# A hybrid decoder layer on one core: the depthwise convolution's taps are moved into earlier projection units, and the samples' taps become one product and one sum per channel tile

## The chip, the cores and the metric

One core of one Trainium2 chip. The time is that of one execution on the device, in microseconds. Five engines work side by side and meet only at semaphores: TensorE (PE, matmuls), VectorE (DVE), ScalarE (ACT), GpSimd (POOL) and SyncE (SP, which issues loads). A kernel's instructions stand in a fixed order on each engine.

## The reference

One layer for a prompt of 1024 tokens and for 8 samples of 4 tokens, with width 1024. What the change touches is the mixer, whose input projection gives q, k, v (512 columns each), and value and gate of a convolution module (512 channels each):

```python
z = h @ p["w_in"]
q, k, v, a, gate = jnp.split(z, [...], axis=-1)
...
attn = combine_branches(outs, lses).reshape(B, T, ATTN_WIDTH)
u = a * jax.nn.sigmoid(gate)
u_ctx = jnp.concatenate([conv_ctx, u], axis=1)          # 30 rows of context in front
c = causal_dwconv(u_ctx, p["conv_w"]) + p["conv_b"]     # width 31, per channel
c = jax.nn.silu(layer_norm(c, p["ln_conv_g"], p["ln_conv_b"]))
mix = jnp.concatenate([rms_norm(attn, ...), rms_norm(c, ...)], axis=-1)
x = x + rms_norm(mix @ p["w_out"], p["g_post_mix"])
```

Behind the mixer come a cross-attention to 256 memory tokens, and a gated feed-forward part with a convolution of width 3. Everything is float32.

## The kernel before

All code is written by hand per engine, with named semaphores: `mark(name, key)` counts one up, `at(name, key)` is the count to wait for.

**Tiles.** Channels lie on the 128 partitions, tokens along the free dimension. The 1056 tokens (1024 of the prompt, 32 of the samples) are worked in 3 chunks of 352 columns. `U` holds the gated values of the prompt, [128, 4 channel tiles, 30 + 1024], `US` those of the samples, [128, 4, 8, 30 + 4], and `C` the convolution's output, [128, 4, 1056]. `cw` holds the taps' weights, [128, 31, 4], so that two taps of a channel tile lie 16 bytes apart.

**The input projection** is a list of 20 units (`order_in`), each one 128 output columns: gate 0, value 0 (`"a"`), gate 1, value 1, and so on to value 3, then four k, four v and four q units. Matmuls are split in three products for accuracy (`whi`, `wlo`), so that a unit has 72 matmuls. `wlo` is a GpSimd subtraction per unit. A unit's three banks are 0 to 2 or 3 to 5 by turns, so TensorE can write a bank when the unit two before has been read from it: gate banks by ScalarE's sigmoid into `U`, value banks by VectorE's product into `U` and `US` (L1563, L1567), k, v and q banks by ScalarE's copies (L570). Behind the unit after a k or v unit TensorE transposes the tile (L997) into banks 6 and 7, in three groups, of which the third needs bank 6 again; VectorE copies them out (`tok_kv`, L1548 and L1550).

**The convolution** is a list of jobs on VectorE, ordered by channel tile, tap and group, `"p"` for the 1024 prompt columns and `"s"` for the 32 sample columns. Each job multiplies the shifted input by the tap's weight and adds it to `C`, so it waits for the job of the same group one tap before. `conv(14)` issues 14 jobs behind each of the twelve k, v and q units (L1571), `conv(2)` two behind each attention step (L1607), until all 248 are done, which is behind the 40th step.

**The attention steps** follow the units: 66 turns for 64 pairs of a query tile i (0 to 7) and a head. Step s has a score product of i + 1 key blocks on TensorE, VectorE's masked maximum (L1484) and its negation (L1594), ScalarE's exponential (L589), TensorE's transposes (L997), ScalarE's copies (L597, L600), and TensorE's product with V, whose result VectorE scales (L1606). On TensorE the order is score s, transposes s - 1, product with V of s - 2. Behind the steps come the sample attention (where `KTS` is first written), the memory part, and the layer norm of `C`.

Memory is placed by hand. `h1hi` and `h1lo`, the split input, are read by all 20 units; later tiles such as `KTS` lie over them.

Of the kernel before, what the change touches and what calls it, by code (L numbers as in the profile page):

```python
# [10 lines left out]
AX = mybir.AxisListType  # L11

P = 128
D = 1024
NT = D // P
SEQ = 1024
BD, TD = 8, 4
NS = BD * TD
NTOK = SEQ + NS
# [8 lines left out]
CT = CC // P  # L28
KW = 31
PAD = KW - 1  # L30
# [73 lines left out]
class Signals:  # L104
# [14 lines left out]
    def mark(self, name, key, by=1):  # L119
        n = SHARED.get(name, name)  # L120
        self.now[n] = self.now.get(n, 0) + by
        assert (name, key) not in self.noted, (name, key)
        self.noted[name, key] = self.now[n]
        return self.sem(name), by
# [5 lines left out]
def layout(nc, ctx, A, O, counts):  # L130
    S = Signals(nc, ctx, counts)
    mark, at = S.mark, S.reached
# [3 lines left out]
    def place(name, off, shape, dt=F32):  # L136
        return nc_at(name, shape, dt, offset=base + off)
# [4 lines left out]
    def sm(name, shape, dt=F32):  # L142
        n = 4
        for s in shape[1:]:
            n *= s
        t = place(name, small[0], shape, dt)
        small[0] += -(-n // 32) * 32
        return t
# [5 lines left out]
    cw = sm("cw", [P, KW, CT])  # L154
# [25 lines left out]
    def mn(name, off, shape, dt=F32):  # L180
        return place(name, MAIN + off, shape, dt)
# [9 lines left out]
    U = mn("U", 119808, [P, CT, PAD + SEQ])  # L191
    US = mn("US", 136672, [P, CT, BD, PAD + TD])
    C = mn("C", 141024, [P, CT, NTOK])
# [13 lines left out]
    attsT = mn("attsT", 51200, [P, AT, NS])  # L207
    usn = mn("usn", 51712, [P, CT, NS])
    KTS = mn("KTS", 55296 - 2048, [P, AT, KEYS])

    mtk = [mn(f"mtk{i}", 67584 + 4096 * i, [P, D]) for i in range(MT)]
    mhi = mn("mhi", 75776, [P, NT, NM], F32R)
# [52 lines left out]
    def g_of(name, m):  # L265
        return prm[:, PRM_AT[name] + m:PRM_AT[name] + m + 1]
# [36 lines left out]
    FIRST_MEM = unit_of["w_mk", 0]  # L303
# [39 lines left out]
    def need_uc(eng, u, c):  # L343

        eng.wait_ge(*at(*(("unit", u) if c == CH - 1 else ("uc", (u, c)))))
# [174 lines left out]
    def _(act):  # L520
# [82 lines left out]
        for b in range(BD + 1):  # L603
            if b < BD:
                for a in range(KTILES):
# [4 lines left out]
                    if n == 0:  # L610
                        act.wait_ge(*at("pv", len(steps) - 1))
                    act.activation(KTS[:, :, a * P:(a + 1) * P], bank[n % 4][:, :].rearrange("p (k n) -> p k n", k=AT), ACT.Copy).then_inc(*mark("kts", n))
                act.wait_ge(*at("smax", b))
# [372 lines left out]
    def _(pe):  # L986
# [139 lines left out]
        def scores(b):  # L1126
# [4 lines left out]
            R = H * TD  # L1131
            for out, rhs in ((bank[4][0:R, 0:512], lambda k: KTS[:, k, 0:512]), (bank[5][0:R, 0:KEYS - 512], lambda k: KTS[:, k, 512:KEYS]),
                             (bank[5][0:R, KEYS - 512:KEYS - 512 + NS], lambda k: KT[:, k, SEQ:NTOK])):
# [344 lines left out]
    def _(dve):  # L1478
        def stt(out, in0, scalar, in1, op0, op1):
            return dve.scalar_tensor_tensor(out=out, in0=in0, scalar=scalar, in1=in1, op0=op0, op1=op1)  # L1480

        def masked_max(out, scores, bias, acc, start):

            return dve.tensor_tensor_reduce(out=out, in0=scores, in1=bias, scale=SCALE, scalar=start, op0=ALU.add, op1=ALU.max, accum_out=acc)  # L1484
# [7 lines left out]
        for i in range(2):  # L1492
            dve.wait_ge(*at("prm_t", 2 + i))
            for k in range(CT):
                ins = dve.tensor_copy(US[:, k, 4 * i:4 * i + 4, 0:PAD], bank[5 + i][:, k * 120:(k + 1) * 120].rearrange("p (b t) -> p b t", b=4))
# [18 lines left out]
                n += 1  # L1514


        jobs = [(k, t, grp) for k in range(CT) for t in range(KW) for grp in "ps"]
        at_job = [0]

        def conv(count):  # L1520
            while count and at_job[0] < len(jobs):
                k, t, grp = jobs[at_job[0]]
                at_job[0] += 1
                count -= 1
                if t == 0:
                    dve.wait_ge(*at("u", (k, "s")))
                    dve.wait_ge(*at("const", "all"))
                else:
                    dve.wait_ge(*at("conv", (k, t - 1, grp)))
                w = cw[:, t, k:k + 1]  # L1530
                if grp == "p":
                    out, src = C[:, k, 0:SEQ], U[:, k, t:t + SEQ]
                else:
                    out, src = C[:, k, SEQ:NTOK].rearrange("p (b t) -> p b t", t=TD), US[:, k, :, t:t + TD]
                if t == 0:
                    ins = dve.tensor_scalar(out, src, w, g_of("conv_b", k), ALU.mult, ALU.add)
                else:
                    ins = stt(out, src, w, out, ALU.mult, ALU.add)
                ins.then_inc(*mark("conv", "end" if at_job[0] == len(jobs) else (k, t, grp)))

        def tok_kv(kind, i):
            dst = KS if kind == "k" else V
# [11 lines left out]
        for kind, i, _ in order_in:  # L1554
            u = unit_of[kind, i]
            if kind == "a":
                for c in range(CH):
                    need_uc(dve, u, c)
                    b = bank[3 * (u % 2) + c]
                    n = SP0 if c == CH - 1 else CW  # L1560
                    cols = U[:, i, PAD + c * CW:PAD + c * CW + n]
                    dve.wait_ge(*at("sig", (i, c)))
                    dve.tensor_tensor(cols, b[:, 0:n], cols, ALU.mult).then_inc(*mark("u", (i, c)))  # L1563
                    if c == CH - 1:
                        dve.wait_ge(*at("sig", (i, "s")))
                        cols = US[:, i, :, PAD:]
                        dve.tensor_tensor(cols, b[:, SP0:CW].rearrange("p (b t) -> p b t", t=TD), cols, ALU.mult).then_inc(*mark("u", (i, "s")))  # L1567
            if before and before[0] in ("k", "v"):
                tok_kv(*before)
            if kind in ("k", "v", "q"):  # L1570
                conv(14)  # L1571
            before = (kind, i)


        dve.wait_ge(*at("tables", "s"))
        for s in range(len(STEPS) + 2):
            if s < len(STEPS):
                i, h = STEPS[s]
                q, n = s % 2, (i + 1) * P
                dve.wait_ge(*at("score", s))  # L1580
                if s >= 2:
                    dve.wait_ge(*at("ptr", s - 2))
                else:
                    dve.wait_ge(*at("unit", FIRST_MEM - 1))
                parts = -(-n // 512)
                for part in range(parts):
                    k0, k1 = part * 512, min(n, part * 512 + 512)
                    w0 = (TT - 1 - i) * P + k0
                    if part:
                        dve.wait_ge(*at("pm", (s, 0)))  # L1590
                    masked_max(Pp[q][:, k0:k1], bank[2 * q + part][:, 0:k1 - k0], wt[:, w0:w0 + k1 - k0], mx[:, q, part:part + 1],
                                    mx[:, q, 0:1] if part else -3e38).then_inc(*mark("pm", (s, part)))
                dve.wait_ge(*at("pm", (s, parts - 1)))
                dve.tensor_scalar(negm[:, q:q + 1], mx[:, q, parts - 1:parts], -1.0, None, ALU.mult).then_inc(*mark("pmax", s))  # L1594
            if 1 <= s <= len(STEPS):
                q = (s - 1) % 2
                dve.wait_ge(*at("pexp", s - 1))
                if s >= 3:
                    dve.wait_ge(*at("att", s - 3))
                dve.reciprocal(rden[:, q:q + 1], den[:, q:q + 1]).then_inc(*mark("prd", s - 1))  # L1600
            if s >= 2:
                i, h = STEPS[s - 2]
                q = s % 2
                dve.wait_ge(*at("pv", s - 2))
                dve.wait_ge(*at("prd", s - 2))
                dve.tensor_scalar(ATT[:, i, h * DH:(h + 1) * DH], bank[6 + q][:, h % 2 * DH:h % 2 * DH + DH], rden[:, q:q + 1], None, ALU.mult).then_inc(*mark("att", s - 2))  # L1606
            conv(2)  # L1607
        dve.tensor_copy(usn[:, :, :].rearrange("p k (b t) -> p k b t", t=TD), US[:, :, :, PAD:]).then_inc(*mark("usn", 0))
        conv(len(jobs))
        for k, n in ((0, PAD), (1, NS)):  # L1610
            dve.wait_ge(*at("cst_t", k))
            dve.tensor_copy(cst[0:n, k, :], bank[6 + k][0:n, :]).then_inc(*mark("cst", k))
# [15 lines left out]
        for b in range(BD):  # L1628
# [21 lines left out]
            v = bank[7][:, 0:AT * 8].rearrange("p (k x) -> p k x", x=8)  # L1650
# [214 lines left out]
        for c in range(CH):  # L1865
            for j in range(FT):
                a, o = aext[j % 2], cv[j % 2]
# [7 lines left out]
                ins = dve.tensor_copy(a[:, 0:2], carry[:, :, j])  # L1875
                if c == CH - 1:
                    ins.then_inc(*mark("actx_p", (c, j)))
                    ins = dve.tensor_copy(sa[:, :, 0:2], sffn[:, :, j].rearrange("p (b t) -> p b t", t=2))
# [3 lines left out]
                for t in range(2):  # L1882
                    w = fw[:, t, j:j + 1]
                    parts = [("p", o[:, 0:n], a[:, t:t + n])] + ([("s", so, sa[:, :, t:t + TD])] if c == CH - 1 else [])
                    for grp, out, src in parts:
                        if t:
                            dve.wait_ge(*at("cvs" if grp == "s" else ("cv" if c < CH - 1 else "cvp"), (c, j, t - 1)))
                        ins = stt(out, src, w, out, ALU.mult, ALU.add)
# [8 lines left out]
                ins = dve.tensor_copy(carry[:, :, j], a[:, n:n + 2])  # L1897
                if c == CH - 1:
                    ins.then_inc(*mark("acar_p", (c, j)))
                    ins = dve.tensor_copy(sffn[:, :, j].rearrange("p (b t) -> p b t", t=2), sa[:, :, 4:6])  # L1900
# [12 lines left out]
                u = unit_of["lin", c, j]  # L1913
# [67 lines left out]
```

## Time and profile before

| | |
|---|---|
| median of 3 runs | 2160.55 us (2148.82 to 2164.36) |
| profiled execution | 2163.04 us, span 2161.1 us |
| busy share of the span: PE / DVE / ACT / POOL | 92% / 51% / 41% / 35% |
| chain that ended last: PE / DVE / ACT | 67% / 20% / 6% |
| prompt taps (L1480, 128x1024) | 120 of them, 154.9 us busy, 1291 ns each |
| sample taps (L1480, 128x32) | 120 of them, 50.4 us busy, 420 ns each |
| mean granted TensorE clock | 0.932 |

The span reaches from the first instruction to the last; the execution's own time is 1.9 us longer. Busy shares are means over stages that are bounded by different engines, so a stage is read by itself: the chain of waits says which engine ended a stretch, the windows how busy each engine was in it and which TensorE clock was granted (1.00 is 2.4 GHz, 0.50 is 1.2 GHz). "Idle before" names the time an engine stood still in front of an instruction and who released it. Spacings are read from start to start, because the recorded ends of two neighbours on an engine overlap a little.

### The profile page before, as it was taken

The page shows a single profiled execution, that of the slowest core. Times are in us where ns is not written, and L with a number is a line of the kernel's source. Part 1 is how long each engine was busy: PE and PEld are TensorE (multiplying, and loading weights), DVE is VectorE, ACT ScalarE, POOL GpSimd, SP SyncE. Part 2 cuts the span into 40 slices and gives each one's busy share as a digit, 9 for nine tenths or more (in the row PEclk, how much of TensorE's full clock was granted, in tenths as well). Part 3 has the DMA queues.
Part 4 walks back from the last instruction along what each step waited for, and adds up shares of the span by engine and source line. Part 5 has one row for each costly group of instructions (what it writes and reads, how often), then busy time and mean ns, then how long its engine had stood idle before and what let it go on. Part 6 is the DMA issues. An engine that isn't in the chain of part 4 may idle for free.

```text
span 2161.1 us, 30206 instructions
## 1 busy us (share of the span) xinstructions
PE 1988.2 (92%) x11926; PEld 1787.2 (83%) x11926; DVE 1098.3 (51%) x1974; ACT 885.7 (41%) x1682; POOL 754.8 (35%) x324
## 2 busy tenths in 40 slices
PE   3999979999899868788899998899999999999999
PEld 2999976677666647787888877899999999998998
DVE  3117997844111134256732457768426872179821
ACT  5211123444211145455555455555435453354543
POOL 1112210000000014344433324456666566655664
PEclk9999985899777679899999999999999999999999
DMA  4111230000433113434444443434444454444543
GB/s 148 30 49 39 80 113 1 1 1 5 167 136 136 68 59 98 158 112 132 123 152 133 129 138 89 118 107 135 132 137 137 133 154 137 137 137 118 159 128 112
DMA packets 348547, 231.28 MB, mean 107 GB/s; under 512 B 7915, under 2 KB 322401, under 8 KB 348399
## 3 DMA queue, kind: packets, MB, share of 16 engines
q1 hardware_dynamic: 342387, 217.84, 33.2%
q10 hardware_dynamic: 6020, 11.51, 1.5%
q8 instruction: 96, 1.57, 0.3%
q14 instruction: 44, 0.36, 0.1%
HBM read 218.24 MB, written 11.50 MB: 106 GB/s over the span
## 4 chain that ended last, share of the span: by engine, by line
PE 67%; DVE 20%; ACT 6%; issue 4%; DMA 1%; SPq 1%; ACTq 0%; POOL 0%; DVEq 0%
PE bank L1000 61%; DVE C L1480 6%; PE bank L997 6%; DVE cv L1480 2%; DVE carry L1897 2%; DVE Y L1480 2%; DVE op_lo L1480 1%; DVE XT L1739 1%; ACT whi L529 1%; DVE Sx L1727 1%; ACT junk L542 1%; DVE cv L1915 1%; SPq L381 1%; ACT cv L907 1%; DVE Ps L1484 0%
## 5 line engine op out<-in xcount | busy, mean ns | idle before, releaser
L516 POOL TENSOR_TENSOR wlo<-raw,whi 128x1024 fp32r<-128x1024 f32 (+1 forms) x312 | 753.6, 2420 | 1387.9 <-ACT whi L529 1387.9
L1000 PE MATMUL bank<-op_hi,whi 128*128 128x352 f32 x1632 | 545.2, 334 | 15.9 <-POOL wlo L516 8.1
L1000 PE MATMUL bank<-op_hi,wlo 128*128 128x352 f32 x1632 | 530.7, 325 | 0.0
L1000 PE MATMUL bank<-op_lo,whi 128*128 128x352 f32 x1632 | 529.8, 325 | 0.0
L529 ACT ACTIVATE whi<-raw 128x1024 fp32r<-128x1024 f32 (+1 forms) x312 | 323.5, 1043 | 275.2 <-DMA raw<-in_w_in_dram 78.3
L1000 PEld LDWEIGHTS bank<-op_hi,whi 128*128 128x128 f32 x1632 | 311.6, 191 | 28.8 <-issue 17.3
L1000 PEld LDWEIGHTS bank<-op_lo,whi 128*128 128x128 f32 x1632 | 312.6, 192 | 0.3
L1000 PEld LDWEIGHTS bank<-op_hi,wlo 128*128 128x128 f32 x1632 | 311.8, 191 | 0.0
L1720 DVE TENSOR_TENSOR Sy<-Sy,SQy 128x352 f32<-128x352 f32 x63 | 40.8, 648 | 292.3 <-ACT SQy L703 292.3
L1000 PE MATMUL bank<-fhi,whi 128*128 128x352 f32 x528 | 171.1, 324 | 0.0
L1000 PE MATMUL bank<-fhi,wlo 128*128 128x352 f32 x528 | 170.7, 323 | 0.0
L1480 DVE SCALAR_TENSOR_TENSOR cv<-aext,fw,cv 128x352 f32<-128x352 f32 (+2 forms) x176 | 142.7, 842 | 47.8 <-ACT aext L913 34.6
L1000 PE MATMUL bank<-h1hi,whi 128*128 128x352 f32 x480 | 156.2, 325 | 0.0
L1480 DVE SCALAR_TENSOR_TENSOR C<-U,cw,C 128x1024 f32<-128x1024 f32 x120 | 154.9, 1291 | 0.0
L1000 PE MATMUL bank<-h1hi,wlo 128*128 128x352 f32 x480 | 154.6, 322 | 0.0
L1000 PE MATMUL bank<-h1lo,whi 128*128 128x352 f32 x480 | 154.5, 322 | 0.0
L1897 DVE COPY carry<-aext 128x2 f32<-128x2 f32 x66 | 122.9, 1862 | 0.0
L589 ACT ACTIVATE Pp<-Pp,negm 128x128 f32<-128x128 f32 (+7 forms) x64 | 49.6, 775 | 132.8 <-DVE negm L1594 132.8
L1000 PEld LDWEIGHTS bank<-fhi,wlo 128*128 128x128 f32 x528 | 99.8, 189 | 0.0
L1000 PEld LDWEIGHTS bank<-fhi,whi 128*128 128x128 f32 x528 | 99.3, 188 | 0.0
L1000 PE MATMUL bank<-KT,QT 64*128 64x512 f32 (+3 forms) x192 | 93.6, 602 | 0.6 <-ACT QT L570 0.6
L1000 PEld LDWEIGHTS bank<-h1lo,whi 128*128 128x128 f32 x480 | 90.8, 189 | 0.0
(265 smaller groups left out, 3035.2 us busy)
## 6 DMA issues: line engine op xcount, KB each, us to landing
raw<-in_w_up_dram SPq DMA_DIRECT2D x132, 512.0 KB, 3.8
raw<-in_w_down_dram SPq DMA_DIRECT2D x48, 512.0 KB, 3.9
raw<-in_w_out_dram SPq DMA_DIRECT2D x24, 512.0 KB, 3.9
raw<-in_w_xq_dram SPq DMA_DIRECT2D x24, 512.0 KB, 4.0
raw<-in_w_xo_dram SPq DMA_DIRECT2D x24, 512.0 KB, 3.9
raw<-in_w_in_dram SPq DMA_DIRECT2D x20, 512.0 KB, 3.9
raw<-in_w_down_dram SPq DMA_DIRECT2D x24, 384.0 KB, 3.4
cached<-in_cache_win_k_dram SPq DMA_DIRECT2D x8, 1024.0 KB, 5.3
```

The costliest lines, as they stand in the source:

```text
L381: sp.dma_start(dst, src).then_inc(*mark(name, key, 16))
L516: pool.tensor_tensor(wlo[u % SLOTS][:, 0:nk, :], raw[u % SLOTS][:, 0:nk, :], whi[u % SLOTS][:, 0:nk, :].bitcast(F32), ALU.subtract).then_i ...
L529: act.activation(whi[v % SLOTS][:, 0:nk, :], raw[v % SLOTS][:, 0:nk, :], ACT.Copy).then_inc(*mark("w_hi", v))
L542: act.activation(junk[0:n, :], xt[i][0:n, hf * 512:(hf + 1) * 512], ACT.Square, accum_out=ssx[0:n, i, hf:hf + 1]).then_inc(*mark("xss", (i ...
L589: act.activation(Pp[s % 2][:, 0:n], Pp[s % 2][:, 0:n], ACT.Exp, bias=negm[:, s % 2:s % 2 + 1], accum_out=den[:, s % 2:s % 2 + 1]).then_inc ...
L907: act.activation(cv[j % 2][:, :], bank[u % 4][:, 0:CW], ACT.Copy, scale=fw[:, 2, j:j + 1]).then_inc(*mark("cv0", (c, j)))
L997: return pe.transpose(out, in_, ident[r:r + n, r:r + n])
L1000: return pe.matmul(out, lhsT, rhs, start=first, stop=last)
L1480: return dve.scalar_tensor_tensor(out=out, in0=in0, scalar=scalar, in1=in1, op0=op0, op1=op1)
L1720: dve.tensor_tensor(Sy[:, :], Sy[:, :], SQy[:, :], ALU.add).then_inc(*mark("ysum", (name, c, m)))
L1727: dve.tensor_tensor(Sx[:, :], Sx[:, :], SQx[m % 2][:, :], ALU.add).then_inc(*mark("xsum", (name, c, m)))
L1897: ins = dve.tensor_copy(carry[:, :, j], a[:, n:n + 2])
```

## The change

The job list holds only the prompt's 124 taps. They are issued behind every unit but the first: 8 behind each gate and value unit, 6 behind each k, v and q unit, and none between the attention steps. Behind the last unit a new block, `conv_samples`, works the samples' taps out per channel tile with three instructions: a product of the overlapping windows of `US` (8 samples, 4 tokens, 31 taps, so 992 elements a partition) with the weights into a new tile `taps`, a sum over the taps into `C`, and the addition of the bias. `taps` lies where `KTS` will be, over a part of `h1lo`, so the block waits for the last unit. Each of the three instructions waits for the one in front of it that it depends on. The mark `("conv", "end")` moves to the block's last instruction.

```diff
--- before.py
+++ after.py
@@ -207,6 +207,7 @@
     attsT = mn("attsT", 51200, [P, AT, NS])
     usn = mn("usn", 51712, [P, CT, NS])
     KTS = mn("KTS", 55296 - 2048, [P, AT, KEYS])
+    taps = mn("taps", 55296 - 2048, [P, NS, KW])
 
     mtk = [mn(f"mtk{i}", 67584 + 4096 * i, [P, D]) for i in range(MT)]
     mhi = mn("mhi", 75776, [P, NT, NM], F32R)
@@ -1514,29 +1515,43 @@
                 n += 1
 
 
-        jobs = [(k, t, grp) for k in range(CT) for t in range(KW) for grp in "ps"]
+        jobs = [(k, t) for k in range(CT) for t in range(KW)]
         at_job = [0]
 
         def conv(count):
             while count and at_job[0] < len(jobs):
-                k, t, grp = jobs[at_job[0]]
+                k, t = jobs[at_job[0]]
                 at_job[0] += 1
                 count -= 1
                 if t == 0:
                     dve.wait_ge(*at("u", (k, "s")))
                     dve.wait_ge(*at("const", "all"))
                 else:
-                    dve.wait_ge(*at("conv", (k, t - 1, grp)))
+                    dve.wait_ge(*at("conv", (k, t - 1)))
                 w = cw[:, t, k:k + 1]
-                if grp == "p":
-                    out, src = C[:, k, 0:SEQ], U[:, k, t:t + SEQ]
-                else:
-                    out, src = C[:, k, SEQ:NTOK].rearrange("p (b t) -> p b t", t=TD), US[:, k, :, t:t + TD]
+                out, src = C[:, k, 0:SEQ], U[:, k, t:t + SEQ]
                 if t == 0:
                     ins = dve.tensor_scalar(out, src, w, g_of("conv_b", k), ALU.mult, ALU.add)
                 else:
                     ins = stt(out, src, w, out, ALU.mult, ALU.add)
-                ins.then_inc(*mark("conv", "end" if at_job[0] == len(jobs) else (k, t, grp)))
+                ins.then_inc(*mark("conv", (k, t)))
+
+        def conv_samples():
+
+            dve.wait_ge(*at("conv", (CT - 1, KW - 1)))
+            dve.wait_ge(*at("unit", FIRST_MEM - 1))
+            for k in range(CT):
+                if k:
+                    dve.wait_ge(*at("conv", ("sum", k - 1)))
+                else:
+                    dve.wait_ge(*at("u", (CT - 1, "s")))
+                shifted = bass.AP(US, k * BD * (PAD + TD), [[CT * BD * (PAD + TD), P], [PAD + TD, BD], [1, TD], [1, KW]])
+                weights = cw[:, :, k:k + 1].rearrange("p (b t a) k -> p b t (a k)", b=1, t=1).broadcast_to([P, BD, TD, KW])
+                dve.tensor_tensor(taps[:, :, :].rearrange("p (b t) a -> p b t a", t=TD), shifted, weights, ALU.mult).then_inc(*mark("conv", ("taps", k)))
+                dve.wait_ge(*at("conv", ("taps", k)))
+                dve.tensor_reduce(C[:, k, SEQ:NTOK], taps[:, :, :], AX.X, ALU.add).then_inc(*mark("conv", ("sum", k)))
+                dve.wait_ge(*at("conv", ("sum", k)))
+                dve.tensor_scalar(C[:, k, SEQ:NTOK], C[:, k, SEQ:NTOK], g_of("conv_b", k), None, ALU.add).then_inc(*mark("conv", "end" if k == CT - 1 else ("bias", k)))
 
         def tok_kv(kind, i):
             dst = KS if kind == "k" else V
@@ -1567,11 +1582,13 @@
                         dve.tensor_tensor(cols, b[:, SP0:CW].rearrange("p (b t) -> p b t", t=TD), cols, ALU.mult).then_inc(*mark("u", (i, "s")))
             if before and before[0] in ("k", "v"):
                 tok_kv(*before)
-            if kind in ("k", "v", "q"):
-                conv(14)
+            if u:
+                conv(8 if kind in ("gate", "a") else 6)
             before = (kind, i)
 
 
+        conv(len(jobs))
+        conv_samples()
         dve.wait_ge(*at("tables", "s"))
         for s in range(len(STEPS) + 2):
             if s < len(STEPS):
@@ -1604,9 +1621,7 @@
                 dve.wait_ge(*at("pv", s - 2))
                 dve.wait_ge(*at("prd", s - 2))
                 dve.tensor_scalar(ATT[:, i, h * DH:(h + 1) * DH], bank[6 + q][:, h % 2 * DH:h % 2 * DH + DH], rden[:, q:q + 1], None, ALU.mult).then_inc(*mark("att", s - 2))
-            conv(2)
         dve.tensor_copy(usn[:, :, :].rearrange("p k (b t) -> p k b t", t=TD), US[:, :, :, PAD:]).then_inc(*mark("usn", 0))
-        conv(len(jobs))
         for k, n in ((0, PAD), (1, NS)):
             dve.wait_ge(*at("cst_t", k))
             dve.tensor_copy(cst[0:n, k, :], bank[6 + k][0:n, :]).then_inc(*mark("cst", k))
```

## Rows read from the trace of the kernel before

**Rows 1.** The chain that ended last, 182 to 316 us: start, us, what.

```profile
182.01 11.65 DVE C L1480 x14
195.06 11.65 DVE C L1480 x14
...
220.68 11.53 PE bank L1000 x72
...
284.64 31.57 DVE C L1480 x41
```

**Rows 2.** Timeline of TensorE, end of a v unit (start us, length us).

```profile
232.05 1.03 PE L997 MATMUL bank<-ident,VT 128*128 128x128 f32 x8
...
233.53 0.40 PE L1000 MATMUL bank<-h1hi,whi 128*128 128x352 f32 x1
```

**Rows 3.** ScalarE in order of time, the last q unit's last bank.

```profile
307.54 0.46 ACT L570 ACTIVATE QT<-bank 128x352 f32<-128x352 f32 x1 [3.35 <-PE bank L1000]
```

**Rows 4.** VectorE in order of time, the first score's maximum.

```profile
317.38 0.28 DVE L1484 CUSTOM_DVE_ANT_0 Pp<-bank,wt 128x128 f32<-128x128 f32 x1
```

**Rows 5.** Windows: stretch, length, busy PE PEld DVE ACT POOL, PEclk, DMA.

```profile
308.00:312.00 4.00, 0.49 (x4) 0.30 (x4) 4.00 (x7) 1.29 (x2) 0.00 (x0) 1.00 0.83 274
312.00:316.00 4.00, 0.00 (x0) 0.00 (x0) 4.00 (x7) 0.00 (x0) 0.00 (x0) 0.58 0.84 316
317.38:333.65 16.27, 12.16 (x36) 8.16 (x36) 15.69 (x54) 5.09 (x23) 0.00 (x0) 0.50 0.00 1
338.00:357.50 19.50, 19.50 (x59) 12.52 (x59) 16.04 (x53) 6.20 (x21) 0.00 (x0) 0.50 0.00 0
357.50:393.00 35.50, 35.50 (x106) 22.50 (x106) 22.18 (x65) 11.11 (x30) 0.00 (x0) 0.50 0.00 0
393.00:434.60 41.60, 39.83 (x226) 28.02 (x226) 36.66 (x110) 19.15 (x47) 0.00 (x0) 0.98 0.00 1
```

**Rows 6.** VectorE in order of time, value units and the first conv pairs.

```profile
80.90 0.53 DVE L1563 TENSOR_TENSOR U<-bank,U 128x352 f32<-128x352 f32 x1 [15.84 <-PE bank L1000]
...
103.79 0.53 DVE L1563 TENSOR_TENSOR U<-bank,U 128x352 f32<-128x352 f32 x1 [14.67 <-PE bank L1000]
...
157.21 0.49 DVE L1563 TENSOR_TENSOR U<-bank,U 128x320 f32<-128x320 f32 x1 [3.29 <-PE bank L1000]
...
158.64 1.28 DVE L1480 SCALAR_TENSOR_TENSOR C<-U,cw,C 128x1024 f32<-128x1024 f32 x1
159.84 0.24 DVE L1480 SCALAR_TENSOR_TENSOR C<-US,cw,C 128x32 f32<-128x32 f32 x1
160.00 1.28 DVE L1480 SCALAR_TENSOR_TENSOR C<-U,cw,C 128x1024 f32<-128x1024 f32 x1
...
162.56 2.39 DVE L1480 SCALAR_TENSOR_TENSOR C<-US,cw,C 128x32 f32<-128x32 f32 x1
```

**Rows 7.** VectorE in order of time, a cross-attention head.

```profile
1110.84 0.42 DVE L1785 TENSOR_REDUCE mx<-bank 128x1 f32<-128x256 f32 x1 [8.82 <-PE bank L1000]
1111.29 0.15 DVE L1787 TENSOR_SCALAR negm<-mx 128x1 f32<-128x1 f32 x1
```

**Rows 8.** GpSimd in order of time.

```profile
162.14 2.76 POOL L516 TENSOR_TENSOR wlo<-raw,whi 128x1024 fp32r<-128x1024 f32 x1 [8.96 <-ACT whi L529]
```

**Rows 9.** Groups of VectorE by form: busy us, mean ns, idle before.

```profile
L1695 DVE TENSOR_TENSOR C<-C,RSC 128x352 f32<-128x352 f32 x24 | 11.0, 520 | 0.2
...
L1878 DVE COPY aext<-sffn 128x16 f32<-128x16 f32 x22 | 3.7, 169 | 0.0
```

**Rows 10.** TensorE in order of time, steps with five key blocks.

```profile
418.30 0.74 PE L997 MATMUL bank<-ident,Pp 128*128 128x128 f32 x5
418.87 1.28 PE L1000 MATMUL bank<-V,PT 128*128 128x128 f32 x10
420.08 1.34 PE L1000 MATMUL bank<-KT,QT 64*128 64x512 f32 x4
421.59 0.74 PE L997 MATMUL bank<-ident,Pp 128*128 128x128 f32 x5 [0.17 <-ACT PT L600]
```

## Prediction

> **What bounds the kernel now.** I began with the chain of waits over the stretch that the change touches. From 182 us on, runs of 14 VectorE conv operations stand in it, 11.65 us each and 13.05 us apart, with a whole TensorE unit of 11.53 us taking its turn once; behind 284.64 us the chain is VectorE's conv alone for 31.57 us [rows 1]. The reader should see two different things there. In the k and v units the two engines are nearly tied: VectorE takes 13.05 us a unit, and TensorE, in a unit whose turned tiles VectorE was already waiting for, takes 11.53 us of products and 1.48 us from the first transpose to the next unit's first product, 13.01 us together [rows 1, 2]. In the q units there are no turned tiles to wait for, TensorE runs ahead, and VectorE is late by itself.
>
> The next question is what this lateness costs. ScalarE takes the last bank of the last q unit at 307.54 us [rows 3], and VectorE takes the first score at 317.38 us [rows 4]. So about 9.8 us lie between, in which TensorE has no work. The windows show what follows: the granted clock is at its upper level (2.4 GHz) in 308 to 312 us, falls in 312 to 316 us after TensorE has stood idle, and stays at the lower level (1.2 GHz, shown as 0.50) until about 393 us [rows 5]. In the attention steps behind that, TensorE has 12.16 us of work in the first 16.27 us, and is then busy without a gap, at the lower clock, from 338 to 393 us. From there to 434.6 us, where the last conv operation has been issued, it is busy 39.83 of 41.60 us [rows 5]. The conv pairs between the steps therefore cost time only at the two ends of that stretch; in its middle TensorE at its lower clock is the bound.
>
> **Moving the prompt taps forward.** There are 124 of them (4 channel tiles, 31 taps). Now a tap of the prompt and one of the samples alternate: 1.36 us a pair, of which the sample operation adds 0.16 us to the start of the next [rows 6]. Without it, a prompt tap waits for the tap in front of it directly. No row shows such a pair of this size; two dependent operations stand in the cross-attention, where a 0.42 us reduction is followed 0.45 us after its start, so 0.03 us behind its end [rows 7]. I take 1.27 + 0.04 = 1.31 us a tap. The ends are 1.20 (spacing of operations that don't depend) and 1.36. So removing 124 sample operations saves VectorE only some 6 us, not 124 times their 0.24.
>
> Gate and value units: VectorE idles there almost wholly (14.67 us before one product) [rows 6]. The change puts 8 taps behind each of 7 units. Two units of TensorE last 22.89 us (80.90 to 103.79 [rows 6]). VectorE gets 16 taps, 21.0 us, three or four products for 1.45 us, and the blocking by GpSimd: when GpSimd's subtraction of 2.76 us starts at 162.14 [rows 8], the sample operation beside it lasts 2.39 instead of 0.24 us [rows 6], 2.15 us more, and there are about two of these per pair of units. Sum 26.8 us against 22.89: VectorE falls behind by about 4 us a pair, for three pairs. It has one unit, 11.45 us, to give before TensorE misses the bank of the unit two before. Followed through tap by tap, with seven GpSimd operations hit, VectorE ends its last first-chunk product at about 169.6 us, where TensorE wants that bank at 157.2 + 11.45 = 168.7 us [rows 6]. I charge 0.9 us (0 to 3.3, by the two ends of the tap).
>
> k, v and q units: 6 taps are 7.9 us, with a collision 10.0, with the three copies of turned tiles 11.4, against TensorE's 13.01. TensorE bounds these units; it gains the difference of 0.04 us in seven of them, at most 0.3, and I take 0.2. In the q units 20 taps remain (124 - 56 - 48) behind the last copies: the unit at 220.68 is the second v unit, so those copies come four units of 13.01 us later, at 272.7 to about 273.5 us; 26.2 us and two collisions more make 304 us. TensorE ends at 307.5, and the cover is 3 us. Each tap that slips past it would cost 1.31 us.
>
> **The sample block.** It waits for the last unit, because the product lies in memory that the units still read, and so all of it stands bare: the first score's maximum is queued behind it on VectorE, ScalarE's exponential waits for that, TensorE's transpose for the exponential. Four times it has a product over 992 elements a partition, a sum of 992 to 32, and a bias addition over 32. No row has these sizes. A product of 352 elements is 520 ns, a copy of 16 is 169 ns [rows 9], 1.045 ns an element more; product: 0.52 + 640 x 1.045 ns = 1.19 us. The sum: the 0.42 us reduction has 256 elements [rows 7]; with 736 more 1.19 us. The bias: 0.15 us for one element [rows 7], 0.18 with 32. With the waits, and 0.08 us overlap at an independent start, 2.55 us a tile, 10.2 us in all. Upper end: one more nanosecond for each of the 992 elements in both operations, 8.3 us more; lower end 8.5 us. I stay at the lower part, because an operation reading 16 elements at a stride of 88 bytes still takes 169 ns [rows 9], so a stride alone isn't dear.
>
> The Trainium skill, "SBUF — State Buffer", in the section "Door 1: The DMA port swizzle", says that accesses which go on to a new line of 16 bytes each time pay a penalty. The weights here step 16 bytes from tap to tap, so this speaks against the change. If it doubled the product's cost an element, the block would be 4.1 us longer and the time 2160 us; that case is inside the first rival. The strided copy disagrees, though it is short.
>
> TensorE's last unit ends at 307.5 - 0.2 + 0.9 = 308.2 us, the first maximum starts at 308.2 + 10.2 = 318.4, where it was at 317.38: **+1.0 us**. So the wait of VectorE's late conv is replaced by one of the same length, and the clock falls as before.
>
> **The steps without conv pairs.** In the first 16.27 us TensorE idles 4.11 [rows 5], of which I leave 1.0 for the first maximum and exponential, which stay. What is late next is TensorE itself, with 12.16 us of work for eight steps. **-3.1 us** (-2 to -4). From 338 to 393 us nothing is gained, as TensorE is busy throughout. Behind the rise: the windows show 1.77 us of idle. A step with five key blocks now takes 3.29 us (418.30 to 421.59); its pieces are 0.57 + 1.21 + about 1.27 (1.34 less the overlap of 0.07) = 3.05 us [rows 10], so over the 13 steps there it could be 0.24 each, 3.1 us. I take **-2.0 us** (-1.5 to -3.1). The tail of the conv behind the steps had nothing left to do, and VectorE's copy of the sample rows and the load of the second cache window wait for the steps' end anyway: 0.
>
> **Sum.** +1.0 - 3.1 - 2.0 = -4.1 us. The profiled execution took 2163.04 us with a span of 2161.1, so it becomes 2158.9, a ratio of 0.998. The median of the three runs is 2160.55, and 0.998 of it is about **2156 us**.
>
> **Rivals.**
> *The block is dear.* It stands between the last unit and the first maximum, with nothing over it. From 14.3 us on, the change is slower than before (10.2 + 4.1). With the product alone at two nanoseconds an element the time is 2160 us; with both long operations so, the block is 18.5 us and the time 2156 + 8.3 = 2164 us, slower than before. For it: overlapping and broadcast reads that no row shows. Against it: the strided copy. 0.20, half of it for the longer block.
> *The clock rises earlier.* The steps start differently packed, and the rise came at 393 us for no reason that a queue gives. If it came at 357 us, up to half of the 35.5 us [rows 5] would go: 2156 - 17.8 = 2138. Against it: TensorE was already busy without a gap from 338 us with the same work, for 55 us, and got no rise. 0.07.
> *The clock rises later.* If it missed the steps up to 434.6 us, their 37 us of pure work would take twice as long: 2193. The same work in the same order goes before it, so 0.05.
> *The move doesn't do what it says*: VectorE is so far behind that taps spill past the last unit. With 1.36 us a tap and a collision more, the bank stall is 3.3 us and the cover of 3 us gone: 2160. 0.06.
>
> **How the numbers follow.** My forecast has 0.62; its own bounds reach from 2151 to 2162. The runs before lie from 2148.82 to 2164.36, so a median moves by some microseconds for no cause. The range is 2141 to 2166: it takes in the dear block and the spill, and leaves out the two cases of the clock. About 1%, 21.6 us, is what a measurement of this kernel can tell from no change. Faster by that needs the early rise nearly in full: 0.06. Slower by that needs the late rise or a block of 36 us: 0.06. Within: 0.88.
>
> **What would show it.** In the changed kernel's trace: prompt taps 1.31 us apart; the products of the second to the fourth value unit ending some 4, 9 and 13 us behind TensorE, with a bank stall of about 1 us near 169 us; k and v units 13.0 us apart; no tap behind the last unit; eight long operations of about 1.2 us each between 308 and 318.4 us; a clock at 0.50 from about 313 to 390 us; the first eight steps about 1.6 us apart; the steps behind the rise without idle. The prediction is wrong if the block is over 14 us or under 8, or if the clock falls or rises at other work than now.

## The result, and the profile after

The changed kernel takes 2174.4 us (median of 9 runs, 2170.32 to 2180.15) against 2162.83 us (9 runs): ratio 1.0062, 95% interval 1.0041 to 1.0082. It is slower by 0.6%, where 0.2% faster was forecast; the interval lies wholly above 1, so the loss is clear of the noise. The profiled execution took 2170.32 us, the fastest of the nine, with a span of 2168.5 us, 7.4 us more than before.

In the same chain of waits as in [rows 1] (start, us, what), the k and v units are now TensorE's alone, and one unit is odd:

```profile
193.53 13.30 PE bank L1001 x72
...
208.34 11.51 PE bank L1001 x72
...
286.58 34.58 PE bank L1001 x216
```

The conv's 31.57 us in front of the steps are gone. But 193.53 is too late: the unit before it had ended near 181 us. TensorE's timeline shows why ("KT" is the k tile that it transposes, and "[11.32 <-DVE KS L1563]" is the time that it stood still first, and what released it):

```profile
180.78 1.03 PE L998 MATMUL bank<-ident,KT 128*128 128x128 f32 x8
...
193.14 0.40 PE L998 MATMUL bank<-ident,KT 128*32 128x128 f32 x1 [11.32 <-DVE KS L1563]
```

The first k tile's third group of transposes waits 11.32 us for VectorE's copy of the first. VectorE's timeline shows what stood in front of that copy:

```profile
168.65 1.34 DVE L1578 TENSOR_TENSOR U<-bank,U 128x352 f32<-128x352 f32 x3
169.92 0.18 DVE L1582 TENSOR_TENSOR US<-bank,US 128x32 f32<-128x32 f32 x1
170.01 22.47 DVE L1481 SCALAR_TENSOR_TENSOR C<-U,cw,C 128x1024 f32<-128x1024 f32 x14
192.40 1.28 DVE L1563 COPY KS<-bank 128x512 f32<-128x512 f32 x2
```

Fourteen taps take 22.47 us: the 8 behind the last value unit and the 6 behind the first k unit. VectorE reaches the copy at 192.40 us; TensorE had been ready for it since before 182. And the windows (columns as in [rows 5]) show that the stall costs twice:

```profile
185.00:189.00 4.00, 0.00 (x0) 0.00 (x0) 3.93 (x3) 1.00 (x1) 2.68 (x1) 0.77 0.00 0
189.00:193.00 4.00, 0.00 (x0) 0.00 (x0) 3.93 (x5) 0.00 (x0) 0.00 (x0) 0.50 0.00 0
193.00:207.00 14.00, 13.86 (x77) 13.85 (x77) 8.01 (x9) 1.06 (x3) 0.00 (x0) 0.84 0.01 1
...
334.57:350.80 16.23, 15.16 (x45) 9.85 (x46) 7.89 (x48) 6.79 (x29) 0.00 (x0) 0.50 0.00 1
350.80:400.00 49.20, 49.20 (x143) 30.96 (x144) 15.79 (x76) 14.97 (x45) 0.00 (x0) 0.50 0.00 0
400.00:443.30 43.30, 43.13 (x246) 30.88 (x245) 21.19 (x91) 21.47 (x52) 0.00 (x0) 0.97 0.01 1
```

TensorE idles, its clock falls to the lower level, and the next unit begins at that level and takes 13.30 instead of 11.5 us. The last q unit's last bank is taken at 321.18 us (307.54 before, [rows 3]), and then the block stands bare, with no work of TensorE over it:

```profile
321.24 1.93 DVE L1550 TENSOR_TENSOR taps<-US,cw 128x992 f32<-128x992 f32 x1 [1.87 <-PE bank L1001]
323.20 1.19 DVE L1552 TENSOR_REDUCE C<-taps 128x32 f32<-128x992 f32 x1
324.43 0.24 DVE L1554 TENSOR_SCALAR C<-C,prm 128x32 f32<-128x32 f32 x1
324.58 1.93 DVE L1550 TENSOR_TENSOR taps<-US,cw 128x992 f32<-128x992 f32 x1
...
334.57 0.29 DVE L1485 CUSTOM_DVE_ANT_0 Pp<-bank,wt 128x128 f32<-128x128 f32 x1
```

That is 3.33 us a channel tile, and the first maximum comes at 334.57 us, 17.2 us later than in [rows 4]. In the steps 8.5 us come back: the chain reaches the last transposes at 533.05 us before and at 541.75 us after, 215.7 and 207.2 us behind the first maximum. TensorE now has 15.16 us of work in 16.23 at their start, and 43.13 in 43.30 around and behind the rise of the clock.

### The profile page after: what moved, and what is told of

It reads as the page before. It is cut to its first block, busy times and chain, and to the rows that moved or that the text cites. A ratio compares the mean times of both kernels' runs of the same rounds, so it can differ in the third digit from the quotient of the medians.

```text
span 2168.5 us, 30091 instructions
## 1 busy us (share of the span) xinstructions
PE 1985.0 (92%) x11926; PEld 1786.9 (82%) x11926; DVE 1113.7 (51%) x1862; ACT 886.1 (41%) x1682; POOL 755.3 (35%) x324
## 4 chain that ended last, share of the span: by engine, by line
PE 70%; DVE 18%; ACT 6%; issue 4%; DMA 1%; SPq 1%; ACTq 0%; POOL 0%; DVEq 0%
PE bank L1001 63%; PE bank L998 6%; DVE C L1481 4%; DVE cv L1481 2%; DVE Y L1481 2%; DVE carry L1912 2%; DVE XT L1754 1%; DVE op_lo L1481 1%; ACT whi L530 1%; DVE Sx L1742 1%; ACT junk L543 1%; SPq L382 1%; DVE cv L1930 1%; ACT cv L908 1%; DVE Sy L1735 0%
## 5 line engine op out<-in xcount | busy, mean ns | idle before, releaser
L1481 DVE SCALAR_TENSOR_TENSOR C<-U,cw,C 128x1024 f32<-128x1024 f32 x120 | 186.5, 1554 | 3.9
L1001 PEld LDWEIGHTS bank<-h1hi,whi 128*128 128x128 f32 x480 | 91.4, 190 | 0.6 <-DVE U L1578 0.5
```

The lines of the kernel that those rows point to most:

```text
L1001: return pe.matmul(out, lhsT, rhs, start=first, stop=last)
```

## The experiments

Each was compared with runs of the kernel before on the same chip. There are 12 runs of each (11 of e5), but only 5 of e8, 4 of e9 and e10, and 5 of e11. "First maximum" is the start of VectorE's first score maximum in the profiled run.

| kernel | median, us | ratio to before, 95% interval | first maximum, us |
|---|---|---|---|
| before | 2162.83 | | 317.38 |
| changed | 2174.4 | 1.0062 (1.0041 to 1.0082) | 334.57 |
| e1_counts | 2165.22 | 1.0002 (0.9985 to 1.0020) | 324.39 |
| e2_weights | 2170.79 | 1.0034 (1.0020 to 1.0049) | 332.23 |
| e3_move_only | 2167.26 | 1.0009 (0.9996 to 1.0022) | 327.30 |
| e4_block_only | 2171.12 | 1.0029 (1.0012 to 1.0046) | 330.44 |
| e5_counts_weights | 2163.65 | 0.9994 (0.9985 to 1.0003) | 323.85 |
| e6_late | 2160.82 | 0.9978 (0.9963 to 0.9994) | 311.58 |
| e7_spread | 2157.54 | 0.9966 (0.9953 to 0.9980) | 311.32 |
| e8_warm | 2142.81 | 0.9892 (0.9873 to 0.9910) | 310.80 |
| e9_warm_less | 2135.12 | 0.9865 (0.9850 to 0.9879) | 309.82 |
| e10_before_warm | 2192.59 | 1.0136 (1.0119 to 1.0153) | 318.86 |
| e11_split | 2125.6 | 0.9826 (0.9809 to 0.9842) | 310.95 |

My theory after the result: 14 taps in front of the first k copies cost 13 us, the strided product some 3. The rival: the bare block is the whole loss.

**e1_counts: fewer taps in front of the first k copies.**

```diff
             if u:
-                conv(8 if kind in ("gate", "a") else 6)
+                conv(7 if u in (1, 3, 5) or FIRST_MEM - 12 < u < FIRST_MEM - 4 else 6)
```

> The changed kernel with other numbers of taps behind each unit and nothing else: 7 and 6 by turns behind the gate and value units, 6 behind the last value unit, 7 behind k and v units, 6 behind q units, so that VectorE reaches the first k tile's copies before TensorE does. Theory (TensorE stands 11 us at the first k tile because 14 taps are queued in front of its copies, and its clock falls there): that stall and the slow unit behind it go, the last unit ends near 307.7 instead of 321.2 us, and the time falls by 13 us against the changed kernel, to about 2161 us, ratio to before 0.998. Rival (the loss is all the sample block, and the lateness only moves the idle time about): no more than 2 us gained, ratio 1.005.

(The first k unit kept 6 taps, not 7.) The ratio falls from 1.0062 to 1.0002, some 13 us; the two intervals don't touch, but leave this number open by about 6 us either way. VectorE now waits for TensorE at the k copies instead of the other way round:

```profile
180.88 1.29 DVE L1563 COPY KS<-bank 128x512 f32<-128x512 f32 x2 [2.98 <-PE bank L998]
...
311.07 1.93 DVE L1550 TENSOR_TENSOR taps<-US,cw 128x992 f32<-128x992 f32 x1
...
324.39 0.29 DVE L1485 CUSTOM_DVE_ANT_0 Pp<-bank,wt 128x128 f32<-128x128 f32 x1
```

The last q bank is taken at 307.40 us, as before the change and 13.8 us sooner than in the changed kernel. But the block starts only at 311.07: of the taps taken from the gate and value units, 4 now stand behind the q units, and they spill 3.6 us past the last unit, which I had not reckoned with. So the first maximum comes 10.2 us sooner. The rival (2 us) falls. This profile is no typical one: it took 2151.36 us, the fastest of twelve, and its windows say why.

```profile
356.00:360.00 4.00, 4.00 (x12) 2.04 (x11) 1.28 (x6) 0.98 (x3) 0.00 (x0) 0.50 0.02 4
360.00:364.00 4.00, 4.00 (x14) 2.70 (x13) 1.71 (x9) 1.22 (x4) 0.00 (x0) 0.50 0.00 0
364.00:368.00 4.00, 3.98 (x19) 2.47 (x17) 1.38 (x6) 2.03 (x6) 0.00 (x0) 0.87 0.00 0
```

The clock rose at about 365 us, in the steps with three key blocks, 41 us behind the first maximum instead of 68 in the changed kernel's profile, with TensorE as busy as there. Between the 17th and the 25th transposes lie 18.95 us here and 29.92 in the changed kernel, with the same work: 11 us by the clock alone.

**e2_weights: the weights next to each other.**

```diff
-    cw = sm("cw", [P, KW, CT])
+    cw = sm("cw", [P, CT, KW])
...
-        dve.tensor_copy(cw[:, :, :].rearrange("p a k -> p (a k)"), bank[7][:, PRM_N:PRM_N + KW * CT])
+        dve.tensor_copy(cw[:, :, :], bank[7][:, PRM_N:PRM_N + KW * CT].rearrange("p (a k) -> p k a", k=CT))
...
-                weights = cw[:, :, k:k + 1].rearrange("p (b t a) k -> p b t (a k)", b=1, t=1).broadcast_to([P, BD, TD, KW])
+                weights = cw[:, k, :].rearrange("p (b t a) -> p b t a", b=1, t=1).broadcast_to([P, BD, TD, KW])
```

> The changed kernel with the taps' weights laid out [channel tile, tap], so that the sample product reads them next to each other instead of 16 bytes apart. Theory (the 16 byte step is what makes the product 1.93 us): the product falls to about 1.19 us, the block from 13.3 to 10.4 us, ratio about 1.005 against 1.006. Rival (the overlapping windows or the broadcast cost it): the product stays at 1.93 us.

Groups of VectorE by form, in the changed kernel and then here (busy us, mean ns):

```profile
L1550 DVE TENSOR_TENSOR taps<-US,cw 128x992 f32<-128x992 f32 x4 | 7.7, 1924 | 1.9 <-PE bank L1001 1.9
```

```profile
L1550 DVE TENSOR_TENSOR taps<-US,cw 128x992 f32<-128x992 f32 x4 | 4.7, 1187 | 1.6 <-PE bank L1001 1.6
```

1924 ns become 1187, with the same overlapping windows and the same broadcast. So the 16 byte step is the whole difference. The trace thus agrees with the Trainium skill ("SBUF — State Buffer", "Door 1: The DMA port swizzle"), that accesses which go on to a new line of 16 bytes each time pay a penalty, which I had set aside. The last q bank and the first maximum are 10.45 us apart, as expected. The ratio falls by 0.0028, 6 us; the two intervals overlap, and hold the expected 3.

**e3_move_only: the old pairs in the new places, no block.**

```diff
-            if kind in ("k", "v", "q"):
-                conv(14)
+            if u:
+                conv(16 if kind in ("gate", "a") else 12)
...
-            conv(2)
```

> One part of the change alone: prompt and sample taps stay pairs as before, but all are moved to the places that the changed kernel gives to its taps (16 jobs behind gate and value units, 12 behind k, v and q units, none between the steps), and there is no sample block. Theory of the queue in front of the k copies: the stall is there, some 3 us longer than in the changed kernel (62 pairs at 0.05 us), so 14 to 15 us. No block stands between the last unit and the first maximum, so TensorE idles only 1 to 2 us there. If the clock then stays at its upper level through the first steps, the time is about 2136 us; if it falls in them all the same, about 2162 us.

The last q bank is taken at 326.15 us, 18.6 us late, more than the 14 to 15 that I had expected; the first maximum follows 1.15 us later, 9.9 us behind that of the kernel before. The steps, now free of conv pairs, give 6.7 us back up to the last transposes, and the ratio of 1.0009 can't be told from 1. The clock falls all the same:

```profile
324.00:328.00 4.00, 2.61 (x18) 2.13 (x16) 2.45 (x9) 1.81 (x3) 0.00 (x0) 1.00 0.16 47
328.00:332.00 4.00, 3.12 (x15) 2.27 (x16) 2.35 (x17) 2.40 (x11) 0.00 (x0) 0.95 1.04 356
332.00:336.00 4.00, 4.00 (x15) 2.88 (x14) 2.13 (x13) 1.96 (x9) 0.00 (x0) 0.50 0.50 189
```

TensorE never stood longer than some 1.3 us at once here, but was busy only 5.73 of the 8 us from 324 to 332. So closing the long gap alone doesn't keep the clock.

**e4_block_only: the block, with the prompt's taps where they were.**

```diff
-            if u:
-                conv(8 if kind in ("gate", "a") else 6)
+            if kind in ("k", "v", "q"):
+                conv(7)
...
-            dve.wait_ge(*at("conv", (CT - 1, KW - 1)))
...
+            conv(1)
```

> The other part alone: the prompt's taps stay where they were (7 behind each k, v and q unit, one behind each step), and the samples are worked out by the block behind the last unit. Theory: VectorE comes to the block as late as it came to the first maximum before, about 316 us, and the block adds its 13.3 us bare, so the first maximum is at about 329.5 us and the time about 2174 us, ratio 1.0055. Rival (the block is free because VectorE's late taps shrink by the sample operations): the first maximum below 322 us, ratio under 1.002.

```profile
317.12 1.93 DVE L1549 TENSOR_TENSOR taps<-US,cw 128x992 f32<-128x992 f32 x1
...
330.44 0.29 DVE L1485 CUSTOM_DVE_ANT_0 Pp<-bank,wt 128x128 f32<-128x128 f32 x1
```

VectorE comes to the block as late as it came to the first maximum, and the block adds its 13.3 us. The rival (below 322 us) falls. The ratio of 1.0029 is less than the 1.0055 expected, since the steps give some of it back: the 40th transposes are at 442.53 us against 434.54 before, 8.0 us, where the first maximum was 13.1 us late.

**e5_counts_weights: both mends, block still bare.** Its edit is those of e1_counts and e2_weights.

> The counts of e1_counts and the weights' layout of e2_weights together, so the block stays bare behind the last unit but without the 16 byte step. If the two losses are separate they add: 13 + 3 us less than the changed kernel, ratio 0.9985 to before; the first maximum some 3 us sooner than in e1_counts, at 321.4 us. If the lateness of VectorE hides the block's cost, ratio 1.000 as in e1_counts.

The ratio is 0.9994, with an interval that holds both forecasts, 0.9985 and 1.000, so the time doesn't settle whether the two losses add. The traces do: from the last q bank to the first maximum lie 14.04 us here and 16.99 in e1_counts, 2.95 less. What is left of the change, a bare block of some 10.4 us behind taps that spill over, is worth nothing against the kernel before. The first maximum is at 323.85 us, not 321.4, because the last q bank was taken 2.4 us later in this run (309.81).

**e6_late and e7_spread: the block in the steps, then the spilling taps too.**

```diff
-    taps = mn("taps", 55296 - 2048, [P, NS, KW])
+    taps = mn("taps", 55296, [P, NS, KW])
...
+            if s in range(40, 48):            # e7_spread alone
+                conv(1)
+            if s - 48 in (0, 3, 6, 9):
+                conv_samples((s - 48) // 3)
```

e7_spread has 4 taps behind each q unit.

> The counts of e1_counts, with the sample block taken off the path: its tile lies elsewhere, and its four tiles are worked behind the attention steps 48, 51, 54 and 57, where VectorE idles more than half of the time. The weights keep their 16 byte step. Theory (bare time is what the block costs): the first maximum comes 13 us sooner than in e1_counts, near 311 us, ratio 0.994. Rival (a block of 3.3 us between two steps delays the next maximum and TensorE with it): up to 4 times 2 us of it come back, ratio 0.998.

> e6_late with 4 instead of 6 taps behind each q unit and the 8 that remain behind steps 40 to 47. In e1_counts the last taps ended some 3.6 us behind the last unit. Theory: the first maximum comes at 308.6 us, 2.7 us sooner than in e6_late, ratio 0.993. Of the clock: in e3_move_only it fell although TensorE stood only 2.3 us, so it should fall here too, about 5 us into the steps. If it stays at the upper level instead, the ratio is near 0.98.

In e6_late the first maximum comes 12.8 us sooner than in e1_counts, but the ratio is 0.9978 instead of 0.994. TensorE's timeline holds part of the rest:

```profile
453.63 1.77 PE L1001 MATMUL bank<-KT,QT 64*128 64x512 f32 x4
455.33 0.98 PE L998 MATMUL bank<-ident,Pp 128*128 128x128 f32 x7
...
461.06 0.95 PE L998 MATMUL bank<-ident,Pp 128*128 128x128 f32 x7 [1.71 <-ACT PT L601]
```

A step with a block takes 5.73 us where its neighbours take 4.15 to 4.50; over the four that is some 6.1 us, and a fifth step, behind the last block, is long too (6.33 against 4.72). From the 40th to the last transposes lie 105.78 us, against 98.47 in the kernel before: 7.3 us in all. So the rival named there held, nearly to the end of its range. e7_spread brings the gap between the last q bank and the first maximum down to 1.14 us and the ratio to 0.9966. Its first maximum was expected at 308.6 us and came at 311.32, as the last q bank was taken only at 310.18 in this run; with overlapping intervals, e7_spread isn't shown to be better than e6_late. The clock fell there at about 314 us, as expected.

**e8_warm and e9_warm_less: TensorE kept at work.** Score products are issued several times into the same bank; the last one stands. This adds work that the result doesn't need.

```diff
                     take(2 * (s % 2) + part, "pm", (s, part))
+                    for again in range(12 if s == 1 else {0: 3, 1: 2, 2: 1}.get(i, 0) if s else 0):
+                        mm(bank[2 * (s % 2) + part][:, 0:k1 - k0], QT[rows, hp, i * P:(i + 1) * P], KT[rows, hp, k0:k1], True, True)
```

> e7_spread with each score product of the first 24 steps issued more than once into the same bank (12 more for step 1, 3 more with one key block, 2 more with two, 1 more with three); the repeats change no result. Theory (the clock falls in the first steps because TensorE has gaps there, and the 70 us behind it are slow only for that reason): it stays at its upper level, and the stretch to the 24th step, 64 us now, takes about 36: ratio about 0.98. Rival (the clock falls for another reason): the repeats run at the lower clock, cost about 36 us more, ratio about 1.01.

> e8_warm with fewer repeats: 12 more for step 1 as there, but 2 more with one key block, 1 more with two, none with three. If the clock stays up all the same, the 24 steps lose the repeats' time, some 0.1 us each with one block, 0.2 with two and 0.7 with three: about 8 us less than e8_warm, ratio 0.986. If the clock falls in the first steps, the ratio is near 0.997 or above.

Windows of e8_warm, then of e9_warm_less (in the dictionary `{0: 2, 1: 1}`):

```profile
308.00:312.00 4.00, 3.45 (x29) 3.16 (x28) 0.45 (x3) 2.24 (x4) 0.00 (x0) 1.00 0.28 81
312.00:316.00 4.00, 3.99 (x32) 3.46 (x31) 1.33 (x9) 1.31 (x6) 0.00 (x0) 1.00 1.04 356
316.00:332.00 16.00, 16.00 (x95) 12.52 (x94) 7.43 (x45) 6.13 (x25) 0.00 (x0) 1.00 0.11 40
332.00:364.00 32.00, 32.00 (x159) 21.27 (x158) 13.84 (x66) 13.06 (x40) 0.00 (x0) 1.00 0.00 1
```

```profile
308.00:312.00 4.00, 3.45 (x32) 3.16 (x31) 0.45 (x3) 2.24 (x4) 0.00 (x0) 1.00 0.51 158
312.00:316.00 4.00, 3.76 (x26) 2.99 (x25) 2.09 (x14) 1.58 (x7) 0.00 (x0) 1.00 1.04 386
316.00:332.00 16.00, 15.91 (x91) 11.76 (x89) 8.58 (x50) 7.32 (x31) 0.00 (x0) 1.00 0.04 14
332.00:364.00 32.00, 31.51 (x170) 20.48 (x169) 16.79 (x75) 16.64 (x46) 0.00 (x0) 1.00 0.00 1
```

The granted clock stays at 2.4 GHz, so the theory held against its rival. From the first to the 25th transposes it takes 51.6 us with all repeats and 42.8 with fewer, against 64.2 in the changed kernel. I had expected 36 with all of them: the repeats themselves fill TensorE (16.00 of 16.00 and 32.00 of 32.00 us), so e8_warm came to 0.9892 and not to 0.98. With fewer, the ratio is the one expected.

**e10_before_warm: the repeats in the kernel before.**

> The kernel before with the repeats of e8_warm and nothing else. There TensorE stands 10 us before the first step, so the clock falls before any repeat runs. Theory (both the gap in front of the steps and the gaps in the first steps must go): the repeats run at the lower clock and cost 15 to 35 us, ratio 1.007 to 1.016, unless the denser first steps bring the clock back. If they do, within the first 8 steps, the ratio is near 0.99 and no change to VectorE's order was needed for it.

```profile
316.00:332.00 16.00, 12.08 (x46) 10.07 (x47) 13.64 (x44) 3.65 (x17) 0.00 (x0) 0.50 0.05 18
332.00:364.00 32.00, 32.00 (x93) 23.35 (x93) 19.26 (x59) 6.55 (x25) 0.00 (x0) 0.50 0.00 1
...
396.00:428.00 32.00, 31.95 (x102) 19.74 (x101) 18.61 (x53) 8.32 (x21) 0.00 (x0) 0.57 0.00 1
```

28 us slower. TensorE stands some 10 us in front of the steps, the clock falls, and the repeats then run at the lower level; TensorE is busy without a gap from 332 us on and the rise comes only at about 423 us. The same repeats gain 15 us over e7_spread (2157.54 to 2142.81) and lose 28 here. Two things differ, the stand in front of the steps and the conv pairs in them, and no run takes them apart.

**e11_split: the samples' work in pieces.** e9_warm_less with e2's layout, and one of the twelve instructions behind each of the steps 48 to 59.

```diff
-            if s - 48 in (0, 3, 6, 9):
-                conv_samples((s - 48) // 3)
+            if s in range(48, 60):
+                conv_samples(*divmod(s - 48, 3))
```

> e9_warm_less with the weights' layout of e2_weights, and with the sample block's twelve instructions one by one behind the steps 48 to 59, instead of three together behind every third step. In e6_late the four steps with a block lasted 5.73 to 5.83 us where their neighbours took 4.15 to 4.50, 6.1 us lost in all. Theory (a lump longer than VectorE's idle time in a step, 1.2 to 1.4 us, reaches TensorE): pieces of 1.19 us fit, the 6 us come back, and the time is about 2129 us, ratio 0.9838. Rival (the samples' work costs the same wherever it lies in the steps): ratio 0.9865 as in e9_warm_less.

VectorE's timeline, a step with a product and one with a sum:

```profile
429.83 1.18 DVE L1552 TENSOR_TENSOR taps<-US,cw 128x992 f32<-128x992 f32 x1
431.33 0.69 DVE L1487 CUSTOM_DVE_ANT_0 Pp<-bank,wt 128x512 f32<-128x512 f32 x1 [0.32 <-PE bank L1001]
...
433.78 1.18 DVE L1555 TENSOR_REDUCE C<-taps 128x32 f32<-128x992 f32 x1
435.28 0.69 DVE L1487 CUSTOM_DVE_ANT_0 Pp<-bank,wt 128x512 f32<-128x512 f32 x1 [0.32 <-PE bank L1001]
```

VectorE is still 0.32 us early for the next score, and the steps with seven key blocks take 3.95 to 4.18 us. From the 40th to the last transposes lie 98.47 us again, against 105.77 in e9_warm_less, so all 7.3 us come back and the rival falls. The run changes two things at once; whether whole blocks with the new layout, some 2.6 us each, would still have reached TensorE wasn't tried. At 0.9826 this is the fastest version, 39 us below the kernel before.

## Why the prediction was wrong, point by point

- **What bounds the kernel** held: k and v units nearly tied (13.01 us of TensorE's own; behind the stall the chain after has unit starts at 208.34 and 221.36), VectorE's lateness in front of the steps, a lower clock from there to the steps with four blocks.
- **Taps**: 1.32 us apart against 1.31 taken. The second to fourth value units' products ended some 4, 9 and 13 us behind TensorE, as written, the last at 170.1 us; the bank stall was about 0.4 us against 0.9.
- **The k units: the step that failed.** I counted "VectorE gets 16 taps" for each pair of units and then went straight to "6 taps are 7.9 us" a unit. The 8 taps behind the last value unit stood in no sum of the k units. With them VectorE reaches the first k copies at 170.1 + 22.4 = 192.4 us, not near 180, and TensorE stands 11.32 us. The lower clock that follows, 1.8 us in the next unit, was named nowhere. e1_counts shows both: with fewer taps in front of the copies the last q bank is taken 13.8 us sooner, and the ratio falls by 0.6%, the whole distance to the kernel before. The rival "the move doesn't do what it says" had VectorE's lateness, but only at the last unit and for some 4 us. At the last unit itself no tap spilled, though the cover was 1.9 us and not 3.
- **The sample block**: 13.4 us from the last q bank to the first maximum instead of 10.2. The sum was right (1.19 us both), the product was 1.92 instead of 1.19. I had weighed the Trainium skill's rule of the 16 byte lines and dropped it for a copy of 16 elements: at 0.74 ns an element they would make 12 of its 169 ns, too few to show. That was the cheaper half of the rival "the block is dear"; the 14.3 us from which it alone would have made the change slower were not reached. (The 8.3 us of its longer half are two operations at twice 1.045 ns an element; one more nanosecond each would be 7.9.)
- **The steps**: -8.5 us against -5.1. The first eight steps gave 3.9 (3.1 forecast): 16.77 us from the first to the ninth transposes became 12.86. The rest lies behind the 25th transposes, 47.9 us to the 40th against 43.5. The idle time there fell from 1.77 to 0.17 us, so the -2.0 of the sum was -1.6. The other 2.8 us or so (an estimate) are the clock's: it rose about one step earlier, some 2.4 us behind the 25th transposes instead of 8.0, which no queue explains. The 0.24 us a step that I gave to the steps with five key blocks wasn't there: 3.29 us is the longest of spacings that alternate, and on average they were 3.21 us before and 3.10 after.
- **Sum**: 13.6 us at the last unit, 3.6 more between it and the first maximum, 8.5 back makes 8.7; the span shows 7.4. The nine runs' median is 4 us above the profiled run, and their ratio, 0.62%, is 13 us; that remainder isn't settled. I had taken 1% as what a measurement can tell here; with nine runs of each kernel the interval is 0.2% to either side.
- **The rivals**: clock earlier or later was put at 0.12 as a difference between the kernels. Neither came in the size that I had named. But the rise moves between executions with the same steps (e1_counts), so the argument that the same work in the same order keeps it in place doesn't hold. What I missed is that a small other change can keep the clock up: the repeats gain 15 us in e8_warm and 22 in e9_warm_less over e7_spread, three to five times the forecast gain.

## What to carry to other kernels

When work is moved along an in-order engine, write down every instruction that stands in front of each operation that another engine waits for, at the seam between two phases above all; a mean load per phase says nothing there. Here a stall of TensorE was paid again at the lower clock behind it (1.8 us behind 11.32), and the light stage that followed a stall stayed slow for 68 us behind its first maximum: look whether TensorE can be kept at work there, but only after the stall itself is gone. Work off the critical path should come in pieces shorter than the gap that hides them: 3.33 us at once reached TensorE here, 1.18 us did not.

## What the runs showed of the hardware

- A VectorE product of 992 float32 elements a partition takes 1187 ns when its second operand is read in a row and 1924 ns when it steps 16 bytes: 0.74 ns an element more (e2_weights, and the changed kernel).
- The clock's rise isn't tied to a place in the program. With the same steps, TensorE busy without a gap behind the first 16 us, it came 41 us behind the first maximum in one execution (e1_counts) and 68 in another (the changed kernel), worth 11 us. The kernel before itself ranges from 2148.82 to 2167.2 us; whether that is the same effect isn't shown, as only one of its runs has a trace.
- The clock fell in e3_move_only with no idle time of TensorE over some 1.3 us, when it was busy 5.73 of 8 us. It held in e9_warm_less, busy 7.21 of 8 us (308 to 316) over the same seam and 15.91 of 16 us behind it.
